# A two-part model on one core: the complex power tables of the state-space mixer built by 24 GpSimd operations in place of 48

## What is computed

```python
lam = lax.complex(a_re, a_im)
dt = jnp.exp(log_step)[:, None]
lam_bar = jnp.exp(lam * dt)
b_bar = ((lam_bar - 1.0) / lam)[:, :, None] * b_mat
bu = jnp.einsum('bsgh,gph->bsgp', uf, b_bar)
# states[t] = lam_bar * states[t-1] + bu[t]
y = jnp.real(jnp.einsum('bsgp,ghp->bsgh', states, c_mat))
```

## Time and profile before

| what | value |
|---|---|
| median of three runs | 1594.6 us (1591.33 to 1596.62) |
| the profiled execution's own time | 1598.35 us |
| its span | 1596.6 us |
| PE busy | 1535.2 us, 96% of the span |
| DVE busy | 1026.1 us, 64% |
| ACT busy | 759.1 us, 48% |
| POOL busy | 222.4 us, 14% |
| mean granted clock of PE | 0.984 of full speed |

### The profile page before, as it was taken

The page is one execution under the profiler, slowest core; times in us unless marked ns, Lnnn a source line. Parts: engine busy times, 40 slices in busy tenths (PEclk is TensorE's granted clock), DMA queues, the critical chain, the costliest instruction groups (busy, mean ns, idle before and its releaser), DMA issues.

```text
span 1596.6 us, 28308 instructions
## 1 busy us (share of the span) xinstructions
PE 1535.2 (96%) x10468; PEld 1409.8 (88%) x10468; DVE 1026.1 (64%) x1391; ACT 759.1 (48%) x1205; POOL 222.4 (14%) x255
## 2 busy tenths in 40 slices
PE   5989999999999999999999999999999999999997
PEld 5989998998988888999988799998999999899996
DVE  6997787766665556555557665555655569565554
ACT  3454634564455445444445254445444457454442
POOL 1695094311002022000000000000000000000000
PEclk9999999979999999999999999999999999999999
DMA  9888874224765655655533355554655545255551
GB/s 347 320 295 287 290 264 124 80 80 141 247 199 176 212 164 195 254 175 195 187 130 106 106 181 177 189 189 140 217 174 188 195 148 145 68 195 175 182 196 40
DMA packets 80563, 294.35 MB, mean 184 GB/s; under 512 B 9051, under 2 KB 9404, under 8 KB 79916
## 3 DMA queue, kind: packets, MB, share of 16 engines
q1 hardware_dynamic: 75728, 274.97, 50.1%
q0 software_dynamic: 3984, 16.21, 3.1%
q10 hardware_dynamic: 780, 2.18, 0.5%
HBM read 289.13 MB, written 3.15 MB: 183 GB/s over the span
## 4 chain that ended last, share of the span: by engine, by line
PE 82%; DVE 9%; ACT 3%; issue 3%; POOL 1%; DMA 1%; SPq 0%; DVEq 0%; ACTq 0%
PE bank L207 72%; DVE w_lo L191 3%; DVE arena L804 2%; PE bank L1972 1%; PE bank L1234 1%; ACT arena L303 1%; PE bank L1985 1%; PE bank L2353 1%; PE bank L2331 1%; POOL stat L342 1%; DMA raw<-panels 1%; PE bank L427 1%; ACT w_hi L185 1%; PE bank L410 1%; PE bank L1220 0%
## 5 line engine op out<-in xcount | busy, mean ns | idle before, releaser
L207 PE MATMUL bank<-h_hi,w_hi 128*128 128x256 f32 x2344 | 673.5, 287 | 5.8 <-DVE w_lo L191 4.4
L207 PE MATMUL bank<-h_hi,w_lo 128*128 128x256 f32 x2344 | 664.4, 283 | 0.0
L207 PE MATMUL bank<-h_lo,w_hi 128*128 128x256 f32 x2344 | 664.3, 283 | 0.0
L191 DVE TENSOR_TENSOR w_lo<-raw,w_hi 128x1024 fp32r<-128x1024 f32 x454 | 548.9, 1257 | 113.9 <-ACT w_hi L185 113.3
L185 ACT ACTIVATE w_hi<-raw 128x1024 fp32r<-128x1024 f32 x458 | 458.0, 1049 | 61.4 <-DMA raw<-panels 31.7
L207 PEld LDWEIGHTS bank<-h_hi,w_hi 128*128 128x128 f32 x2344 | 450.2, 192 | 20.8 <-issue 6.8
L207 PEld LDWEIGHTS bank<-h_lo,w_hi 128*128 128x128 f32 x2344 | 450.5, 192 | 5.7 <-issue 1.9
L207 PEld LDWEIGHTS bank<-h_hi,w_lo 128*128 128x128 f32 x2344 | 450.2, 192 | 0.0
L646 DVE TENSOR_TENSOR arena<-arena,bank 128x256 f32<-128x256 f32 x132 | 55.2, 419 | 253.6 <-PE bank L207 180.0
L207 PE MATMUL bank<-w_hi,f_hi 128*128 128x512 f32 x528 | 208.6, 395 | 3.5 <-DVE f_lo L651 3.5
L207 PE MATMUL bank<-w_hi,f_lo 128*128 128x512 f32 x528 | 207.5, 393 | 0.0
(11 more groups left out here) (329 smaller groups left out, 1392.8 us busy)
## 6 DMA issues: line engine op xcount, KB each, us to landing
raw<-panels SPq DMA_DIRECT2D x458, 512.0 KB, 4.6
arena<-ada SPq DMA_DIRECT2D x64, 512.0 KB, 5.4
arena<-ada POOLq DMA_DIRECT2D x8, 512.0 KB, 3.8
arena<-rows POOLq DMA_DIRECT2D x4, 512.0 KB, 4.4
spectrum<-arena POOLq DMA_DIRECT2D x2, 1024.0 KB, 8.3
arena<-spectrum POOLq DMA_DIRECT2D x1, 2048.0 KB, 18.5
X<-x_in SPq DMA_DIRECT2D x1, 1024.0 KB, 5.7
arena<-decay ACTq DMA_DIRECT2D x2, 512.0 KB, 5.2
```

The lines of the kernel that those rows point to most:

```text
L191: dve.tensor_tensor(w_lo[:, slot, :], raw[:, slot, :], w_hi[:, slot, :].bitcast(F32), ALU.subtract).then_inc(lo_ready, 1)
L207: last = pe.matmul(out_ap, a, b, start=start and n == 0, stop=stop and n == 2)
```

## The change

Real and imaginary parts are now handled by one operation where they are multiplied by the same factor. A call is two wide multiplications (both parts by the real factor, both by the imaginary factor) into two temporary tables, then one subtraction and one addition. The square of `lam_bar` is computed first, in five operations of 128x16. The last two powers of each table then come from the first two in one call of double width. The temporary tables need more room and lie where the near map will lie, so the clearing of the near map moves behind the powers, and ACT waits for both `powers_ready` before it writes there.

```diff
-        power_tmp = region(21504, 3, 256)
+        power_tmp = region(22528, 2, 1024)
...
-        def times_complex(pool, order, out_r, out_i, in_r, in_i, re, im):
-
-            ta, tb, tc = [by_channel(power_tmp[:, j, :]) for j in range(3)]
-            pool.tensor_tensor(ta, in_r, wide(re, 16), ALU.mult)
-            pool.tensor_tensor(tb, in_i, wide(im, 16), ALU.mult)
-            order(pool.tensor_tensor(tc, in_r, wide(im, 16), ALU.mult))
-            order(pool.tensor_tensor(out_r, ta, tb, ALU.subtract))
-            order(pool.tensor_tensor(ta, in_i, wide(re, 16), ALU.mult))
-            order(pool.tensor_tensor(out_i, tc, ta, ALU.add))
...
+        def times_complex(pool, order, out, both, re, im):
+
+            n = both.shape[3]
+            shape = [P, 2, STATE_TILES, n]
+            by_re, by_im = [power_tmp[:, j, 0:2 * STATE_TILES * n].rearrange("p (i s c) -> p i s c", i=2, c=n)
+                            for j in range(2)]
+            pool.tensor_tensor(by_re, both, re.unsqueeze(1).unsqueeze(3).to_broadcast(shape), ALU.mult)
+            order(pool.tensor_tensor(by_im, both, im.unsqueeze(1).unsqueeze(3).to_broadcast(shape), ALU.mult))
+            pool.tensor_tensor(out[:, 0, :, :], by_re[:, 0, :, :], by_im[:, 1, :, :], ALU.subtract)
+            order(pool.tensor_tensor(out[:, 1, :, :], by_im[:, 0, :, :], by_re[:, 1, :, :], ALU.add))
...
-            order(pool.memset(near_map[:, :, :], 0.0))
             order(pool.tensor_tensor(pr(DT), pr(RAD), pr(COS), ALU.mult))
             order(pool.tensor_copy(pr(XR), pr(LI)))
+            pool.tensor_tensor(pr(T0), pr(DT), pr(DT), ALU.mult)
+            pool.tensor_tensor(pr(T1), pr(XR), pr(XR), ALU.mult)
+            order(pool.tensor_tensor(pr(T2), pr(DT), pr(XR), ALU.mult))
+            pool.tensor_tensor(pr(LR), pr(T0), pr(T1), ALU.subtract)
+            order(pool.tensor_tensor(pr(LI), pr(T2), pr(T2), ALU.add))
             pool.wait_ge(ssm_loaded, 32)
...
+            times_complex(pool, order, b_of(3, 4), raw, pr(CR), pr(CI))
+            times_complex(pool, order, b_of(2, 3), b_of(3, 4), pr(DT), pr(XR))
+            times_complex(pool, order, b_of(0, 2), b_of(2, 4), pr(LR), pr(LI))
             pool.sem_inc(powers_ready, 1)
...
+            times_complex(pool, order, c_of(0, 1), c_raw, pr(DT), pr(XR))
+            times_complex(pool, order, c_of(1, 2), c_of(0, 1), pr(DT), pr(XR))
+            times_complex(pool, order, c_of(2, 4), c_of(0, 2), pr(LR), pr(LI))
+            order(pool.memset(near_map[:, :, :], 0.0))
             pool.sem_inc(powers_ready, 1)
...
             act.wait_ge(map_in_psum, 1)
+            act.wait_ge(powers_ready, 2)
```

More of the change, by code:

```diff
@@ L1031, in by_channel, with powers_of @@
             return part.rearrange("p (s c) -> p s c", c=c)
-        def times_complex(pool, order, out_r, out_i, in_r, in_i, re, im):
-            ta, tb, tc = [by_channel(power_tmp[:, j, :]) for j in range(3)]
-            pool.tensor_tensor(ta, in_r, wide(re, 16), ALU.mult)
-            pool.tensor_tensor(tb, in_i, wide(im, 16), ALU.mult)
-            order(pool.tensor_tensor(tc, in_r, wide(im, 16), ALU.mult))
-            order(pool.tensor_tensor(out_r, ta, tb, ALU.subtract))
-            order(pool.tensor_tensor(ta, in_i, wide(re, 16), ALU.mult))
-            order(pool.tensor_tensor(out_i, tc, ta, ALU.add))
-        def power_of(table, part, j):
-            return table[:, part, :, 16 * j:16 * j + 16]
+        def times_complex(pool, order, out, both, re, im):
[7 more added lines that the diff above has]
+            order(pool.tensor_tensor(out[:, 1, :, :], by_im[:, 0, :, :], by_re[:, 1, :, :], ALU.add))
+        def powers_of(table, lo, hi):
+            return table[:, :, :, 16 * lo:16 * hi]
         def tables_pool(pool, order):
@@ L1052, in tables_pool @@
             load_gain(pool, 0)
-            order(pool.memset(near_map[:, :, :], 0.0))
             order(pool.tensor_tensor(pr(DT), pr(RAD), pr(COS), ALU.mult))
             order(pool.tensor_copy(pr(XR), pr(LI)))
-            pool.wait_ge(ssm_loaded, 32)
[L1057 to L1062, removed]
+            pool.tensor_tensor(pr(T0), pr(DT), pr(DT), ALU.mult)
[3 more added lines that the diff above has]
+            order(pool.tensor_tensor(pr(LI), pr(T2), pr(T2), ALU.add))
+            pool.wait_ge(ssm_loaded, 32)
+            raw, c_raw = [ssm_raw[:, 2 * j:2 * j + 2, :].rearrange("p i (s c) -> p i s c", c=16) for j in range(2)]
+            b_of, c_of = [lambda lo, hi, t=t: powers_of(t, lo, hi) for t in (b_powers, c_powers)]
+            times_complex(pool, order, b_of(3, 4), raw, pr(CR), pr(CI))
+            times_complex(pool, order, b_of(2, 3), b_of(3, 4), pr(DT), pr(XR))
+            times_complex(pool, order, b_of(0, 2), b_of(2, 4), pr(LR), pr(LI))
             pool.sem_inc(powers_ready, 1)
[L1064 to L1067, removed]
+            times_complex(pool, order, c_of(0, 1), c_raw, pr(DT), pr(XR))
+            times_complex(pool, order, c_of(1, 2), c_of(0, 1), pr(DT), pr(XR))
+            times_complex(pool, order, c_of(2, 4), c_of(0, 2), pr(LR), pr(LI))
+            order(pool.memset(near_map[:, :, :], 0.0))
             pool.sem_inc(powers_ready, 1)
```

## The result

The changed kernel is slower. Its median is 1606.97 us over four runs (1604.83 to 1609.0) against 1592.96 us for the kernel before timed beside it. The ratio is 1.0085, with a 95% interval from 1.0060 to 1.0111. Timed twice more, it gave 1.0069 (1.0042 to 1.0096) and 1.0063 (1.0040 to 1.0086). The three intervals share 1.0060 to 1.0086, which is 10 to 14 us. I forecast 1603.5 us, or 9 us more than the 1594.6 us of before.

A forecast was written before the change was run, and what follows sets the result against it. PE bounds the kernel, but before 117.78 us DVE's losses count: 22.5 us less 2.0 hidden is 20.5, against 11.1 now, taken as 9 more. 1594.6 + 9 = 1603.6, say 1603.5; range 1597 to 1609.

The forecast's parts named there:

- The price goes by the columns: DVE's L191 beside POOL's powers: each POOL operation costs 0.46 us at 256 columns, 0.94 at 512, 1.88 assumed at 1024.
- The larger sum of 27 us: POOL's powers by the skill's two-input figure: 27 us in place of 22.5, for a loss of about 14 us.
- All of it falls ahead of the seam: Seam: PE's w_lo wait ending at 117.78. All 24 operations fall before it, losing 20.5 us against 11.1.
- Nothing is gained back behind the seam, and nothing is lost: After 117.78 PE is the bound: the 18 operations gone from there are worth nothing, and PE cannot catch up.
- a sign against me: At and after PE's wait ending at 117.78: the forecast is wrong if the shift there shrinks behind it.
- Squaring, clearing, ACT's wait: POOL's five squarings and moved clearing, ACT's wait at the near map: nothing on the path; clearing 1.84 us if POOL were.
- The waits of PE: First feed-forward stage: PE's waits for `w_lo` would sum to 10 us or more instead of 4.4.
- The fixed toll: Rival, POOL's powers: a wide operation costs DVE 0.46 us like a narrow one, gaining 2.1 us, 1592.5; chance 0.07.
- DVE gets two turns: Rival: DVE runs two operations between POOL's, some 15 of 24 before 117.78; 1595.6, or 1599 halfway; chance 0.13.
- Nothing measurable: Rival, whole kernel: something unseen absorbs DVE's lateness, time 1594.6 plus or minus 3; chance 0.07.
- the clock rival: Rival, PE around 117.78: more stretches at the lower clock add 2 to 4 us, 1606 to 1608; chance 0.13.

The follow-up runs named there:

- e2_moves: The kernel before with its 48 narrow operations, plus the moved clearing, the five squarings and ACT's second wait: ratio 0.9993 to the kernel before.
- e3_one_power: The changed kernel with one power at a time, 32 operations and none of 1024 columns: ratio 1.0059 to the kernel before.
- e1_again: The changed kernel once more without edit, in more rounds: ratio 1.0069 (1.0042 to 1.0096) to the kernel before.
- e9_again: The changed kernel a third time without edit, in rounds of its own: ratio 1.0063 (1.0040 to 1.0086) to the kernel before.

## Why the prediction was right

*The price goes by the columns.* Right, and this decides the sign. At 512 columns the price had been read from the trace. At 1024 it was an assumption, 1.88 us. An L191 beside such an operation takes 2.93 us against 1.22 alone, by the list of L191 in the changed kernel between 104.5 and 107:

```profile
L191 DVE TENSOR_TENSOR w_lo<-raw,w_hi x2: 2925/2928/2932, 104.1 to 107.0; 128x1024 fp32r<-128x1024 f32 x2
```

The columns are the least, middle and largest duration in ns. The price is 1.71 us, 9% under my term, so four of them make 0.7 us of the sum. The larger sum of 27 us, which the prediction gave beside its own, needs some 2.2 us for such an operation and does not fit this row. Three L191 in a row took 6.29 us (forecast: 6.3) and at most 7.45 (forecast: up to 9), since only two of the three met operations of 1024 columns.

*All of it falls ahead of the seam.* Right. POOL ended its powers at 113.28 (forecast: near 113), in 47 us (45 to 49), before the fifth tile's three L191 at 114.68. DVE needed 118.12 - 65.81 = 52.3 us to the fifth L646, so it lost 52.3 - 32.1 = 20.2 us; I had 20.5. The seam came 9.2 us later; I had 9.

*Nothing is gained back behind the seam, and nothing is lost.* Right in its main part. The 18 operations that left that stretch were worth nothing. But the shift shrank behind the seam in the first trace, from 9.2 to 7.6 us, and I had named that as a sign against me. What the prediction had left out is the clock: the four slow microseconds behind the seam were part of the time before, and a later clock fall can take their place or not. In the kernel before the clock fell behind the seam, in this trace of the change before the seam at 127, as these rows of stretches have it (us; busy of PE, PEld, DVE, ACT, POOL; clock; DMA share, GB/s):

```profile
114.00:118.00 4.00, 4.00 (x12) 3.12 (x11) 4.00 (x4) 0.00 (x0) 3.82 (x4) 0.57 0.75 237
118.00:122.00 4.00, 4.00 (x35) 3.95 (x34) 3.96 (x6) 3.44 (x4) 3.77 (x7) 1.00 0.93 338
...
126.00:130.00 4.00, 3.79 (x29) 3.33 (x28) 4.00 (x5) 2.27 (x5) 0.00 (x0) 1.00 0.61 222
```

In the two repeats it fell behind the seam too, and the shift stayed at 9.2 us. Which of the two an execution does is not in my sum, so the good fit of 9 to 9.2 is in part luck.

*Squaring, clearing, ACT's wait: nothing.* Right; e2_moves shows it in the trace and in the timing.

*The waits of PE.* Wrong in its split. I expected 10 us or more for `w_lo`. Those waits are 4.0, 6.9 and 5.9 us in the three traces, and another 5.4, 5.8 and 5.4 us are waits for `f_lo`, which I had not named. Together they are 9.4, 12.6 and 11.3. In DVE's program L651 stands behind an L804, and so it is late as well where that is blocked: in the second tile L804 takes 2.60 us from 84.06, L651 starts at 86.59, and PE's wait for `f_lo` ends at 88.20.

*The rivals.* The fixed toll falls by e3_one_power. "DVE gets two turns" falls by POOL's end at 113. "Nothing measurable" falls by the timing. The median of the first timing, 1606.97, lies in the range of the clock rival, 1606 to 1608, and 0.6 us above my own widened range, which ends at 1604.9 + 1.5 = 1606.4. But the clock as an addition of 2 to 4 us on top of the shift is not in the traces: the part of the distance that is not waits grew by 1.0 to 2.7 us, and that is inside the 7.6 and 9.2. The clock does enter that median, by another place than the rival had it, as follows.

*The size.* The traces give 7.6, 9.2 and 9.2 us. The timings give 14, 11 and 10 us, and each interval reaches down to 9.6 us or less. The executions on record explain most of the difference. Those of every kernel here fall into two groups by PE's mean granted clock, and the group with 0.986 or less takes 5 to 8 us more. Medians, with the number of executions:

| kernel | clock 0.987 or more | clock 0.986 or less |
|---|---|---|
| before, timed with e1_again | 1592.3 (17) | 1598.8 (12) |
| the change, e1_again | 1601.2 (3) | 1607.6 (3) |
| e3_one_power | 1599.6 (5) | 1605.8 (7) |
| before, timed with e9_again | 1592.8 (14) | 1598.6 (3) |
| the change, e9_again | 1600.8 (3) | 1606.9 (3) |

Like compared with like, the change costs 8.9 and 8.8 us in the second timing and 8.0 and 8.3 in the third, and e3_one_power costs 7.3 and 7.0. That is what the first stage shows in the traces. In the first timing all four executions of the change have 0.984 or less. The clocks of the four of the kernel before are not on record, but three of their times (1590.92 to 1594.6) are those of the other group. So the mix made up most of the 5 us above the forecast.

The traces show where the groups part, long behind the tables. These are the same stretch in the first trace of the change and in e1_again, one program:

```profile
330.00:340.00 10.00, 10.00 (x50) 10.00 (x49) 4.97 (x9) 8.11 (x26) 0.04 (x1) 0.50 0.35 115
330.00:340.00 10.00, 10.00 (x94) 10.00 (x93) 8.29 (x15) 6.85 (x23) 2.38 (x3) 1.00 0.43 128
```

The six traces with a mean clock of 0.986 or less all have 10 us at 0.50 between 320 and 350 us, and in the six others no such stretch is under 0.83. The kernel before and the change are both found in either group. Open is only whether the change makes the slower group more frequent: it has 10 of 16 executions there and the kernel before 28 of 80, which leaves it open. If these shares hold, it would add an estimated 1.7 us on average, (0.63 - 0.35) x 6.3.

## What to carry to other kernels

When two engines exclude each other and the price goes by the columns, as here, fewer and wider operations on the one in the background do not reduce what the other loses. They bring the same loss forward in time and bunch it, so ask first at which moment the foreground engine can bear it. Here the table of C was not needed until long behind the seam, and one wait that held it back took away nearly the whole loss of the change: 7 to 8 us by the traces, 12 by the timings, 10 to 11 like compared with like. And where executions fall into groups, compare within a group: the mix moved the first ratio by some 5 us. Lastly, add up lateness along the way: the consumer pays for the worst moment, even if the producer is ahead again at the end.

## What was unexpected of the hardware

Operations of POOL that only write left DVE's two-operand operations at 3.48 us for three, beside clearings of up to 1024 columns, while ones that read took them to 7.45 us. The Trainium skill, "SBUF — State Buffer", in the section on the two separate sides, says that a DVE instruction with two SBUF inputs contends only with a GpSimd instruction that reads SBUF, and these runs agree with it.

The same program, run three times under the profiler, had PE wait 9.4, 12.6 and 11.3 us in the same stretch, and yet the seam came 69.2, 69.3 and 69.3 us after POOL's first DMA issue. The waits before it do not add up to the shift. In the first trace POOL's powers started 8.2 us after that issue, because the tables landed late (66.02 against 57.83). In the second they started 7.0 us after it (64.11 against 57.10), and in the third too (65.19 against 58.18). This 1.2 us did not move the seam. The three differ in when PE's clock fell: before the seam in the first, and behind it in the others, where the 60 matmuls took 10.24 and 10.26 us in place of 8.78. Whether the earlier start of POOL had a part in that was not tested.
